# First steps of the second FFN and of the MLP by row tile, and context tiles turned before a fourth weight unit

## What is computed

```python
# first block, layer l (x rows; in layer 0 the context rows h_c go the same way)
h_x = h_x + gm * rms_norm(yx, norm_g[l, 1])
fx = conv_ffn(modulate(rms_norm(h_x, norm_g[l, 2]), shf, scf),
              ffn_w_up[l], ffn_conv_w[l], ffn_conv_b[l], ffn_w_down[l])
h_x = h_x + gf * rms_norm(fx, norm_g[l, 3])

def conv_ffn(u, w_up, conv_w, conv_b, w_down):
    val, gate = jnp.split(u @ w_up, 2, axis=-1)
    return (jax.nn.silu(dwconv3(gate, conv_w, conv_b)) * val) @ w_down

# second block
x = x + token_mixer(rms_norm_2(x, norm_mix_g[l]), w_in[l], ...)
x = x + squared_relu_mlp(rms_norm_2(x, norm_mlp_g[l]), w_up[l], w_down[l])
```

## Time and profile before

| | |
|---|---|
| median of three runs | 1793.3 us |
| the profiled execution | 1789.4 us, span 1787.5 us, mean granted TensorE clock 0.998 |
| TensorE matmul | 98% of the span busy, 9819 instructions |
| TensorE weight loads (beside the matmuls) | 83% |
| VectorE, ScalarE, GpSimd | 65%, 47%, 5% |
| DMA | 282.39 MB, 158 GB/s in the mean |
| chain that ended last | TensorE 93%, ScalarE 3%, VectorE 2% |

### The profile page before, as it was taken

The page is one execution under the profiler, slowest core; times in us unless marked ns, Lnnn a source line. Parts: engine busy times, 40 slices in busy tenths (PEclk is TensorE's granted clock), DMA queues, the critical chain, the costliest instruction groups (busy, mean ns, idle before and its releaser), DMA issues.

```text
span 1787.5 us, 26212 instructions
## 1 busy us (share of the span) xinstructions
PE 1754.1 (98%) x9819; PEld 1489.0 (83%) x9819; DVE 1160.8 (65%) x1532; ACT 845.1 (47%) x1232; POOL 85.3 (5%) x160
## 2 busy tenths in 40 slices
PE   7999999999999999999999999899999999999998
PEld 6778788787788888888888888899889887879987
DVE  5867767676477788644356556666675695775555
ACT  5344343442565433333245556665555646554454
POOL 3010010100000110000000000000001000000000
PEclk9999999999999999999999999999999999999999
DMA  9654555545265576332323222455556554546664
GB/s 338 223 157 146 170 155 163 162 143 171 77 247 177 156 218 188 118 97 88 113 83 97 81 76 87 156 188 180 185 176 193 168 155 153 190 137 207 183 190 128
DMA packets 155406, 282.39 MB, mean 158 GB/s; under 512 B 12923, under 2 KB 86771, under 8 KB 155184
## 3 DMA queue, kind: packets, MB, share of 16 engines
q1 hardware_dynamic: 138672, 223.69, 39.7%
q0 software_dynamic: 16640, 57.42, 10.7%
HBM read 276.83 MB, written 4.23 MB: 157 GB/s over the span
## 4 chain that ended last, share of the span: by engine, by line
PE 93%; ACT 3%; DVE 2%; issue 1%; SPq 1%; DMA 0%; DVEq 0%; ACTq 0%
PE ps L623 29%; PE ps L624 28%; PE ps L625 28%; PE ps L944 1%; PE ps L951 1%; PE ps L1245 1%; PE ps L1224 1%; PE ps L901 1%; PE ps L772 0%; DMA raw<-in_ret_w_in 0%; PE ps L975 0%; SPq L530 0%; ACT arena L2421 0%; PE ps L1235 0%; ACT wh L1719 0%
## 5 line engine op out<-in xcount | busy, mean ns | idle before, releaser
L2630 DVE TENSOR_TENSOR wl<-raw,wh 128x1024 fp32r<-128x1024 f32 (+1 forms) x381 | 445.9, 1180 | 360.1 <-ACT wh L1719 357.9
L1719 ACT ACTIVATE wh<-raw 128x1024 fp32r<-128x1024 f32 (+2 forms) x377 | 384.8, 1026 | 577.9 <-PE ps L625 565.6
L623 PE MATMUL ps<-uh,wh 128*128 128x256 f32 (+1 forms) x1360 | 435.4, 320 | 6.7 <-DVE spare L2652 4.2
L625 PE MATMUL ps<-uh,wl 128*128 128x256 f32 (+1 forms) x1360 | 432.4, 318 | 0.0
L624 PE MATMUL ps<-ul,wh 128*128 128x256 f32 (+1 forms) x1360 | 432.3, 318 | 0.0
L623 PE MATMUL ps<-wh,uh 128*128 128x512 f32 (+1 forms) x772 | 289.6, 375 | 0.0
L623 PEld LDWEIGHTS ps<-uh,wh 128*128 128x128 f32 x1360 | 259.4, 191 | 28.9 <-issue 8.1
L624 PE MATMUL ps<-wl,uh 128*128 128x512 f32 (+1 forms) x772 | 282.3, 366 | 0.0
L625 PE MATMUL ps<-wh,ul 128*128 128x512 f32 (+1 forms) x772 | 282.1, 365 | 0.0
L625 PEld LDWEIGHTS ps<-uh,wl 128*128 128x128 f32 x1360 | 259.4, 191 | 17.3
L624 PEld LDWEIGHTS ps<-ul,wh 128*128 128x128 f32 x1360 | 259.5, 191 | 16.7
(11 more groups left out here) (368 smaller groups left out, 1626.7 us busy)
## 6 DMA issues: line engine op xcount, KB each, us to landing
raw<-in_ffn_w_up SPq DMA_DIRECT2D x176, 256.0 KB
arena<-in_ada_w POOLq DMA_DIRECT2D x80, 512.0 KB, 4.3
raw<-in_w_in SPq DMA_DIRECT2D x60, 512.0 KB
raw<-in_ret_w_in SPq DMA_DIRECT2D x48, 512.0 KB
raw<-in_ffn_w_down SPq DMA_DIRECT2D x40, 512.0 KB
raw<-in_ret_w_out SPq DMA_DIRECT2D x32, 512.0 KB
raw<-in_w_up SPq DMA_DIRECT2D x32, 512.0 KB
raw<-in_w_down SPq DMA_DIRECT2D x32, 512.0 KB
```

The lines of the kernel that those rows point to most:

```text
L623: pe.matmul(o, lh, rh, start=first, stop=False)
L625: return pe.matmul(o, ll, rh, start=False, stop=last)
L1719: T.mark(act.activation(wh[:, j, 0:size], raw[:, j, 0:size], ACT.Copy), hi_done)
L2630: T.mark(vec.tensor_tensor(wl[:, j, 0:size], raw[:, j, 0:size], wh[:, j, 0:size], ALU.subtract), lo_done)
```

## The change

The second FFN's and the MLP's first steps take the mixer's form. What was the mixer's own is made common: `turn_first`, `first_by_tiles`, `finish_first`, `split_early`, `tile_highs`, `tile_lows` and `apply_tile`. Three of the first step's four units are split ahead (`up_unit`, `mlp_unit`). Since these two stages want features on the partitions, the result's tokens are copied from PSUM (`keep_tokens`, tile 0 on ScalarE, tile 1 on VectorE) and turned by 8 transposes behind the first unit of the second step (`turn_tokens` in `step_turning`), and the first step is read behind that. The second FFN's scale and shift are applied per tile and feature block, four blocks on VectorE (`shift_tile`) and four on ScalarE (`shifted_highs`). The loops over steps are one round shorter. In the attention the context tiles are turned after unit 2 of the first pass. The two semaphores of the residual's loads become one, `residual_loaded`.

```diff
@@ tensor
-                    elif j == 3:
+                    elif j == 2:
                         pe.wait_ge(y_gated, 8)
                         turn_part(10, norm_b[1][2:4], heads_v)
-            turn_normed(5, 8, 3)
-            with pe.Fori(0, 5) as i:
...
+            def turn_first():
+                turned_norms[0] += 1
+                tiles_half[0] = open_group()
+                keep_clock(ps[:, tiles_half[0] + 3, 384:TOK], 5)
+                turn_tile(0)
+                keep_clock(ps[:, tiles_half[0] + 3, 384:TOK], 12)
+            def first_by_tiles(unit):
...
                         if t:
                             mm.then_inc(unit_used, 1)
+                        elif j == SLOTS - 1:
+                            mm.then_inc(tile_done, 1)
                         elif j == 2:
                             turn_tile(1)
+            def turn_tokens(half, kept):
+                pe.wait_ge(tokens_kept, kept)
+                for t in range(2):
+                    for m in range(4):
+                        mm = pe.transpose(ps[:, half + m, t * P:(t + 1) * P], tokens[:, t, m * P:(m + 1) * P], ident[:, :])
+                mm.then_inc(turned, 1)
...
+            turn_first()
+            step_turning(first_by_tiles(up_unit), 2)
+            with pe.Fori(0, 4) as i:
...
-            turn_normed(0, 5, 3)
-            with pe.Fori(0, 4) as i:
+            turn_first()
+            step_turning(first_by_tiles(mlp_unit), 4)
+            with pe.Fori(0, 3) as i:
@@ scalar
+            def shifted_highs(t, hb):
+                cols = slice(t * P, (t + 1) * P)
+                act.wait_ge(turned, Q.now() + 2)
+                Q.base += 2
+                for f in range(4, KD):
+                    T.mark(act.activation(normed[:, f, cols], ps[:, hb + 2 * t + 1, (f - 4) * P:(f - 3) * P], ACT.Identity,
+                                          scale=acol[:, 0, f:f + 1], bias=shift(0, f)), act_evac if (t, f) == (1, KD - 1) else act_own)
+                    if f == 5:
+                        tile_high(t, 0)
+                T.settle()
+                T.mark(act.activation(uh[:, 4:KD, cols], normed[:, 4:KD, cols], ACT.Copy), u_high)
+            def keep_tokens(half, done):
+                act.wait_ge(tile_done, done)
+                T.mark(act.activation(tokens[:, 0, :], ps[:, half, :], ACT.Copy), tokens_kept)
+            keep_tokens(first_half, 2)
+            split()
+            act.wait_ge(turned, Q.next() + 1)
+            conv_ffn(0, SEQ, first % 2, first_half)
@@ vector
+            def shift_tile(t, hb, scale0):
+                cols = slice(t * P, (t + 1) * P)
+                if t:
+                    vec.wait_ge(turned, Q.next() + 1)
+                Q.base += 1
+                for f in range(4):
+                    T.mark(vec.tensor_scalar(normed[:, f, cols], ps[:, hb + 2 * t, f * P:(f + 1) * P], acol[:, 0, f:f + 1],
+                                             mcols(0, scale0 - 8 + f, 1), ALU.mult, ALU.add), u_half if f == 3 else vec_own)
+                tile_lows(t)
+            def keep_tokens():
+                hb = step_full()
+                T.mark(vec.tensor_copy(tokens[:, 1, :], ps[:, hb + 1, :]), tokens_kept)
+                return hb
+            def finish_first(gain0, scale0, early):
+                early(range(0, 2))
+                row_scales(gain0, scale0)
+                half = 4 * (par.next() % 2)
+                gate_y(half, 0, whole[0], vec_own)
+                add_gated(0, whole)
+                gate_y(half + 2, 1, parted[0], vec_own)
+                early(range(2, 3))
+                norm_rows(0, whole)
+                gate_y(half + 3, 1, parted[1], emptied)
+                return group_full()
...
+            hb = finish_first(48, 32, lambda units: split_early(up_unit, units))
+            shift_tile(0, hb, 32)
+            add_gated(1, parted)
+            split(units=range(3, 4))
+            norm_rows(1, parted)
+            shift_tile(1, hb, 32)
+            act_read()
+            tick(emptied)
+            first = par.now()
+            hb = keep_tokens()
+            split()
+            vec.wait_ge(turned, Q.next() + 1)
+            conv_ffn(0, SEQ, first % 2, hb)
...
+            split_early(mlp_unit, range(0, 3))
             vec.wait_ge(rows_done, 4)
             add_plain(0, 0, 2)
...
+            keep_tokens()
+            split()
+            square_hidden(0)
+            Q.base += 1
```

More of the change, by code:

```diff
@@ L2137, in wait_residual, with split_early, tile_high @@
                 act.wait_ge(h_ready, 3 * projections[0] - 2 + part)
+            def split_early(unit, step, units):
+                act.wait_ge(lo_done, (step - 1) * SLOTS + 1)
+                for j in units:
+                    act.wait_ge(raw_loaded[j], W.now() * 32 + 32)
+                    T.mark(act.activation(unit(j)[0], raw[:, j, :], ACT.Copy), hi_done)
+            def tile_high(t, b):
+                cols = slice(t * P, (t + 1) * P)
+                halves[0] += 1
+                act.wait_ge(u_half, halves[0])
+                T.mark(act.activation(uh[:, 4 * b:4 * b + 4, cols], normed[:, 4 * b:4 * b + 4, cols], ACT.Copy), u_high)
@@ L2332, in _ @@
             S.base += 2
-            finish_rows()
+            finish_first(lambda units: split_early(up_unit, S_UP1, units))
             shift0[0] = 24
-            prep()
-            first = par.now()
-            with act.Fori(0, 5) as i:
+            norms[0] += 1
+            act.wait_ge(acol_ready, norms[0])
+            tiles_half = 4 * (par.next() % 2)
+            shifted_highs(0, tiles_half)
+            split(units=range(3, 4))
+            for _ in norm_second():
+                pass
+            shifted_highs(1, tiles_half)
+            first = par.now()
+            first_half = 4 * (par.next() % 2)
+            S.base += 1
+            keep_tokens(first_half, 2)
+            split()
+            act.wait_ge(turned, Q.next() + 1)
+            conv_ffn(0, SEQ, first % 2, first_half)
+            with act.Fori(0, 4) as i:
                 for c, n in ((W, 2), (S, 2), (par, 2), (F, 2)):
@@ L2354, in _ @@
             shift0[0] = None
[L2356 to L2387, removed]
+            finish_first(lambda units: split_early(first_unit, S_MIX, units))
             par.next()
@@ L2566, in _ @@
             roots_next()
+            split_early(mlp_unit, S_MUP, range(0, 3))
             rows_full(0)
@@ L3131, in finish_rows, with split_early, tile_lows @@
                 norm_rows(1, parted)
+            def split_early(unit, units):
+                for j in units:
+                    vec.wait_ge(hi_done, W.now() * SLOTS + (j + 1))
+                    h, l = unit(j)
+                    T.mark(vec.tensor_tensor(l, raw[:, j, :], h, ALU.subtract), lo_done)
+            def tile_lows(t):
+                cols = slice(t * P, (t + 1) * P)
+                T.settle()
+                for b in range(2):
+                    highs[0] += 1
+                    vec.wait_ge(u_high, highs[0])
+                    T.mark(vec.tensor_tensor(ul[:, 4 * b:4 * b + 4, cols], normed[:, 4 * b:4 * b + 4, cols], uh[:, 4 * b:4 * b + 4, cols], ALU.subtract), u_low)
@@ L3392, in _ @@
             take_gates(2, 2)
-            finish_rows(48, 32)
-            prep(32)
-            with vec.Fori(0, 5) as i:
+            hb = finish_first(48, 32, lambda units: split_early(up_unit, units))
+            shift_tile(0, hb, 32)
+            add_gated(1, parted)
+            split(units=range(3, 4))
+            norm_rows(1, parted)
[4 more added lines that the diff above has]
+            hb = keep_tokens()
+            split()
+            vec.wait_ge(turned, Q.next() + 1)
+            conv_ffn(0, SEQ, first % 2, hb)
+            with vec.Fori(0, 4) as i:
                 for c, n in ((W, 2), (S, 2), (par, 2), (F, 2), (E, 2)):
@@ L3757, in _, with square_hidden @@
             tick(emptied)
-            split(units=range(0, 1))
+            tiles_half = group_full()
+            apply_tile(0, tiles_half)
+            split(units=range(3, 4))
             norm_rows(1, parted)
-            prep(None)
+            apply_tile(1, tiles_half)
+            tick(emptied)
+            def square_hidden(k):
+                act_read()
+                v = hid3[:, ds(k, 4), :]
+                T.mark(vec.tensor_tensor(v, v, v, ALU.mult), emptied)
             def read_hidden(k):
```

176 lines of the change are left out of this document (102 added, 74 removed).

## The result

| | kernel before | kernel after |
|---|---|---|
| median, us (14 runs each) | 1792.72 | 1796.66 |
| lowest to highest, us | 1788.18 to 1793.48 | 1794.76 to 1798.77 |
| after / before | | 1.0026, interval 1.0018 to 1.0033 |
| profiled execution, us (its span) | 1789.4 (1787.5) | 1795.24 (1793.3) |

The changed kernel is 3.9 us slower. The first fence holds the busy times of the page after; the lines that answer to it are the earlier trace rows.

The account below looks back on a forecast made before the run. TensorE, busy 98% of the span, was taken to bound the kernel. Attention -2.1, second FFN +3.0 and MLP +1.8 sum to +2.7, which on 1793.3 gives 1796.0 us; range 1790.3 to 1799.5.

Parts of the forecast that it names:

- Context tiles, -2.1: Attention: turning the context tiles ahead of the fourth unit starts the second pass earlier, saving 2.1 us (ends 0 and 2.3).
- Second FFN, +3.0: Second FFN's first step: ends at 1154.0 as before, then pause 2.2 and token turning 0.9: +3.0 us, ends +0.5 and +5.
- Pause of 2.2 each: Start of step two, second FFN and MLP: TensorE waits for VectorE's split, queued behind tile 1's token copy; 2.2 us, ends 1.9 to 2.6.
- MLP, +1.8: MLP's first step: early splits delay tile 0's residual addition 2.8 us; with pause and token turning +1.8 us, ends +0.5 and +3.5.
- a byte count of the queue: MLP: SyncE's loads bring 6.2 us x 255 GB/s = 1.58 MB, three raw units, by 1589.7.
- Rival D: MLP early splits: raw units 1.5 us later than the byte count, or slower scaled copies; +4.5 to +6, 1797.8 to 1799.3; chance 0.10.
- Rival A: Pauses lower TensorE's clock, one in three at 1.5 us each; +1.5 or +3.0, 1797.5 to 1799.0; chance 0.22.
- The sum: All three places together: -2.1 + 3.0 + 1.8 = +2.7 us.
- Rival C: Second FFN and MLP both come down to the mixer's 17.9 us; 1786 to 1790.4; chance 0.12.
- the case against it: Against Rival C: attention's projection frees tile 0 only its last half-step early, and shift makes eight copies of two.

## Why the prediction was right

The forecast was 1796.0 us, 2.7 above before and so just inside 0.2%, with nearly equal chances for within 0.2% and for slower. 1796.66 was measured, 0.26% above before by the ratio and so just outside. That the two times differ by only 0.7 is partly luck: the forecast started from the 1793.3 of three runs, and the median of fourteen is 1792.72. The change itself was forecast at +2.7 and measured at +3.9. By its steps:

- **Context tiles, -2.1.** Measured -2.19 in the traces and -1.75 alone. The transposes came at 949.33, the fourth unit at 951.30 and the second pass at 954.18, without the wait of 0.2 that the forecast had for the second tile.
- **Second FFN, +3.0.** Measured +3.03. Counted from the projection's end, tile 0 was turned at 4.87 us (forecast 5.06), the first matmul came at 9.98 (10.06), the step ended at 23.73 (23.8), and step two began at 25.97 (25.96). TensorE's wait before tile 1's pass was 1.10 as forecast. The turning of tokens was 0.8 against 0.9. All this is one execution, and its clock matched the one that was forecast. Seven profiled kernels have this form with the full filler. In four the first matmul came 9.9 to 10.0 us behind the projection's end; in three nearly all of the filler ran at half the clock (4.7 to 4.9 us, 3.6 in the changed kernel's trace), and the matmul came at 11.1 to 11.4. TensorE's timeline of the kernel with filler in the pauses shows such a case:

```profile
1135.49 4.92 PE L785 MATMUL ps<-ident 128*128 128x128 f32 x24
```

The old form has such a second outcome too: in three of six profiles it took 28.1 us to step two's second unit instead of 26.7, with a low stretch over the first step's matmuls. The window of the kernel with the attention's edit alone shows it (columns as the earlier trace rows):

```profile
1141.60:1145.00 3.40, 3.40 (x19) 3.40 (x20) 2.99 (x5) 2.27 (x4) 0.00 (x0) 0.60 0.14 33
```

So +3.03 is one pair out of a spread of more than 1 us. The other steps:

- **Pause of 2.2 each.** Idle 2.08 and 0.16 around it, at both sites, and gone when two splits stood ahead of the copy. The cause was named rightly: a wait in VectorE's queue, not a lack of time on VectorE.
- **MLP, +1.8.** The term that was mis-sized; measured +2.29. Of its steps only the first is off: tile 0 was turned 1.88 us behind the projection's end instead of 1.36. From there 7.11 us to tile 1 (7.1 forecast) and 2.08 of idle time held. I had the three units landed by a byte count of the queue, 5.3 us ahead of the projection's end, and the addition 2.8 us later than today. ScalarE waited 0.96 and 0.70 us for the loads of the second and third unit, and the third released its copy only 4.4 us ahead of the end (1594.11 against 1598.48), 0.9 later than the byte count; the addition came 3.3 later. From there to the rows the forecast had 3.8 us, and it was 3.76. The filler that I had covering the delay was shorter than it by so much. This is a part of Rival D: units 0.9 us late where it had 1.5, and 0.5 us of cost.
- **Rival A** was no rival but an addition. The forecast had one chance in three at 1.5 us for each pause, counted from three idle times of a single trace. Filler in the pauses gave 2.4 us, and in 4 of the 7 places in profiles where a pause stood open, about half the clock (0.50 to 0.57) stood behind it. Of the idle times that it counted, the one ahead of 1142 was followed by a low stretch in 3 of 6 profiles. In the changed kernel's own profiled execution it was behind neither pause.
- **The sum.** The parts add to +3.1, the medians differ by +3.9, and the interval of the ratio goes down to +3.2. A net loss to the clock does not make the difference: the changed kernel's 0.9974 is no lower than the 0.9969 to 0.9971 before. The open pauses do cost clock, but the change also takes away idle times that could lower it: the attention's 2.32 us, followed by a low stretch in one of the two profiles that have it, and the 2.05 at the MLP, followed by one in the earlier trace rows. The parts hold such a stretch: the +2.29 at the MLP is against 1.5 us of low clock before. Without it they add to +4.6, and the mean clocks give some 0.7 back, which is +3.9. This is an estimate from the clocks, uncertain by about 1 us; no run of its own shows it.
- **Rival C** failed, in the main as the case against it said: the second FFN's first step took 23.73 us and the MLP's 18.2 (1598.48 to 1616.68), where the mixer's takes 17.9. The MLP did come near it; the second FFN, with its scaled copies and late gating, did not.

## What to carry to other kernels

When a step is put ahead of another, look at each in-order engine for the first instruction that waits for the whole step's end, and count what is queued behind it. Here a copy that nobody needed for 3 us held the split that TensorE needed at once, and putting two splits ahead of it turned 3.9 us slower into 2.2 us faster. Of those 2.2, the attention's edit gives 1.75 by itself. Where early work is moved ahead of the critical chain, order it by when its data land, and put what waits for the late loads behind what the chain needs. A gain in place can be hidden in the median by the clock behind an idle time; fill the idle time before judging a gain of 1 or 2 us.

## What the runs showed of the hardware

An idle time of TensorE of about 2 us is followed by a stretch of matmuls at half the clock in some executions only, in the same code. Behind the mixer's 1.93 us it was so in 6 of 10 profiles (0.53 over 3.3 us in the fence above), behind the open pauses of 2.08 us in 4 of 7 places, and behind the old second FFN's 2.20 us in 3 of 6. With 16 filler instructions in the idle time it was so in none of 10 places. Such a stretch costs some 1.5 us: 3.3 us at 0.53 hold 1.75 us of work at full clock, and 17 matmuls ran in it where 27 ran in the 3.4 us before. The Trainium skill (TensorE: Matmul & The Clock Gate, What's actually happening) has TensorE throttled unless activity releases it. By that rule the filler helps, as it did here: 0 of 10 places against 4 of 7 open pauses. Why the same idle time is followed by full clock in other executions, no run here shows.
